# Gate matrices of the dense tokens: from one fp32 product a token to three bf16 products a token

## What is computed

```python
s1 = jnp.einsum('thd,kd->thk', q[:, :, 0], sub_k1)
s2 = jnp.einsum('thd,kd->thk', q[:, :, 1], sub_k2)
v1, i1 = lax.top_k(s1, PEER_TOPK)
v2, i2 = lax.top_k(s2, PEER_TOPK)
...
top_s, top_pos = lax.top_k(cand, PEER_TOPK)
eidx = jnp.take_along_axis(cand_idx, top_pos, axis=-1)   # i1 * 128 + i2
gate = jax.nn.softmax(top_s, axis=-1)
act = jax.nn.gelu(jnp.einsum('thkd,td->thk', expert_u[eidx], xb))
y = jnp.einsum('thk,thkd->td', gate * act, expert_v[eidx])
```

## Time and profile before

| | us |
|---|---|
| three runs | 3722.89, 3715.84, 3708.44 |
| median | 3715.84 |
| span of the profiled execution | 3715.8 |
| its TensorE, busy | 3517.8 (95%) |
| its Vector engine, busy | 2481.2 (67%) |
| its GpSimd, busy | 1842.5 (50%) |
| its ScalarE, busy | 1361.9 (37%) |

### The profile page before, as it was taken

The page is one execution under the profiler, slowest core; times in us unless marked ns, Lnnn a source line. Parts: engine busy times, 40 slices in busy tenths (PEclk is TensorE's granted clock), DMA queues, the critical chain, the costliest instruction groups (busy, mean ns, idle before and its releaser), DMA issues.

```text
span 3715.8 us, 61775 instructions
## 1 busy us (share of the span) xinstructions
PE 3517.8 (95%) x21277; PEld 3348.0 (90%) x21277; DVE 2481.2 (67%) x5400; ACT 1361.9 (37%) x1938; POOL 1842.5 (50%) x1172
## 2 busy tenths in 40 slices
PE   7999999999999999999888689999999999999998
PEld 7999999999999999999773359999999999999998
DVE  3342597777775777775678543679697876777774
ACT  3322343534444333333221353344435353333332
POOL 3434456555655555552541234456565655555551
PEclk9999999999999999999998699999999999999999
DMA  3222367877788999994346322467777879999982
GB/s 131 80 69 91 103 188 247 277 247 262 262 281 274 298 310 313 324 320 154 99 116 179 105 74 91 136 193 249 268 240 277 274 282 277 297 326 311 329 295 97
DMA packets 392484, 812.36 MB, mean 219 GB/s; under 512 B 52104, under 2 KB 249672, under 8 KB 384888
## 3 DMA queue, kind: packets, MB, share of 16 engines
q1 hardware_dynamic: 171600, 458.35, 37.0%
q0 software_dynamic: 64608, 230.73, 18.1%
q10 hardware_dynamic: 156048, 120.37, 11.0%
HBM read 695.39 MB, written 112.74 MB: 217 GB/s over the span
## 4 chain that ended last, share of the span: by engine, by line
PE 66%; DVE 16%; DMA 7%; issue 4%; ACT 2%; POOL 2%; SPq 2%; another core or an unknown queue 0%; ACTq 0%; DVEq 0%; POOLq 0%
PE acc L638 42%; PE acc L625 15%; DMA rows<-u_in,expertP 4%; PE misc L774 3%; DVE rows L1838 3%; DMA raw<-slabs_in 2%; POOL w_lo L2274 1%; DVE misc L1773 1%; DVE route L1777 1%; DVE hot_gate L1876 1%; PE misc L814 1%; ACT w_hi L1104 1%; DVE work L1716 1%; DVE keyi L1724 1%; PE misc L843 1%
## 5 line engine op out<-in xcount | busy, mean ns | idle before, releaser
L2274 POOL TENSOR_TENSOR w_lo<-raw,w_hi 128x1024 fp32r<-128x1024 f32 x365 | 892.6, 2446 | 1079.8 <-ACT w_hi L1104 1078.6
L638 PE MATMUL acc<-h_hi,w_hi 128*128 128x416 f32 x3072 | 1097.7, 357 | 0.2 <-POOL h_lo L2316 0.2
L638 PE MATMUL acc<-h_lo,w_hi 128*128 128x416 f32 x3072 | 1085.9, 353 | 0.0
L638 PE MATMUL acc<-h_hi,w_lo 128*128 128x416 f32 x3072 | 1081.2, 352 | 0.0
L1104 ACT ACTIVATE w_hi<-raw 128x1024 fp32r<-128x1024 f32 x617 | 653.3, 1060 | 1090.0 <-DMA raw<-slabs_in 1045.4
L638 PEld LDWEIGHTS acc<-h_hi,w_hi 128*128 128x128 f32 x3072 | 581.2, 189 | 8.5 <-POOL h_lo L2316 0.6
L638 PEld LDWEIGHTS acc<-h_hi,w_lo 128*128 128x128 f32 x3072 | 581.9, 189 | 7.4
L638 PEld LDWEIGHTS acc<-h_lo,w_hi 128*128 128x128 f32 x3072 | 581.3, 189 | 3.9
L1955 DVE TENSOR_TENSOR w_lo<-raw,w_hi 128x1024 fp32r<-128x1024 f32 x252 | 325.4, 1291 | 206.1 <-ACT w_hi L1104 205.5
L1838 DVE CUSTOM_DVE_ANT_0 rows<-acc,rows 128x1024 f32<-128x1024 f32 (+1 forms) x224 | 273.4, 1221 | 205.9 <-DMA rows<-u_in,expertP 183.7
L638 PE MATMUL acc<-y_hi,w_hi 128*128 128x416 f32 x1024 | 362.1, 354 | 10.3 <-DVE y_lo L1947 4.3
(11 more groups left out here) (349 smaller groups left out, 5549.4 us busy)
## 6 DMA issues: line engine op xcount, KB each, us to landing
raw<-slabs_in SPq DMA_DIRECT2D x617, 512.0 KB
act_d<-gelu SPq DMA_DIRECT2D x256, 208.0 KB
gate_d<-gout SPq DMA_DIRECT2D x52, 1024.0 KB
abuf<-act_d ACTq DMA_DIRECT2D x32, 1664.0 KB
gbuf<-gate_d ACTq DMA_DIRECT2D x30, 1664.0 KB
unit<-ck_in SPq DMA_DIRECT2D x72, 128.0 KB
vquad<-cv_in SPq DMA_DIRECT2D x64, 128.0 KB
unit<-ck_in ACTq DMA_DIRECT2D x56, 128.0 KB
```

Of the source, the lines that this page charges most:

```text
L638: last = pe.matmul(acc[:, 0, par, 0:ND], w[:, c, :], m(c), start=c == 0 and w is w_hi[r] and m is m_hi, stop=c == KC - 1 and w is w_lo[r])
L2274: pool.tensor_tensor(w_lo[r][:], raw[r][:], w_hi[r][:].bitcast(F32), ALU.subtract).then_inc(lo_done, 1)
```

## The change

`idxT` and `gateT` become bf16, and `gateT` holds three bf16 parts of the gate. `gate_parts`, new and run once in each block after `gateT`'s first part has come, makes parts two and three by subtraction. A bf16 count `iota8` in SBUF, in which each of the numbers 0 to 127 stands eight times, is made once a layer and takes the place of `count_row`. The one-hots are bf16 with the token as the innermost of the free dimensions, so that the 8 tokens of a step are done by one tensor_tensor: two comparisons and three products, five instructions of 128x1024 elements. TensorE reads one token's operands out of them with a step of 8 elements (16 bytes) and adds three products into the same PSUM place. The differences `topd` and `topdS` are now written where the exponential is taken (the names stand for that place).

```diff
-        idxT = take("idxT", [P, 2, ND])
-        gateT = take("gateT", [P, ND])
+        idxT = take("idxT", [P, 2, ND], BF16)
+        gateT = take("gateT", [P, 3, ND], BF16)
+        iota8 = take("iota8", [P, P, TG // 2], BF16)
...
-        hot1 = [take(f"hot1_{r}", [P, HG, P]) for r in range(2)]
-        hot_gate = [take(f"hot_gate{r}", [P, HG, P]) for r in range(2)]
+        hot1 = [take(f"hot1_{r}", [P, P, HG], BF16) for r in range(2)]
+        hot_gate = [take(f"hot_gate{r}", [P, 3, P, HG], BF16) for r in range(2)]
...
-                            last = pe.matmul(misc[:, q, j * P:(j + 1) * P], hot1[par][:, t, :],
-                                             hot_gate[par][:, t, :], start=True, stop=True)
+                            for part in range(3):
+                                last = pe.matmul(misc[:, q, j * P:(j + 1) * P], hot1[par][:, :, t],
+                                                 hot_gate[par][:, part, :, t], start=part == 0, stop=part == 2)
...
-            count_row = misc[:, 3, 0:P]
+            rest = misc[:, 3, 0:P]
...
-                dve.tensor_copy(count_row, iota[:]).then_inc(dve_step, step.up())
...
+            def gate_parts(b):
+                t0 = max(b * P, D0)
+                c0, c1 = t0 - D0, (b + 1) * P - D0
+                gate = misc[:, 2, 2 * P + t0 - b * P:3 * P]
+                left = rest[:, t0 - b * P:P]
+                dve.tensor_tensor(left, gate, gateT[:, 0, c0:c1], ALU.subtract).then_inc(dve_step, step.up())
+                dve.wait_ge(dve_step, step.at)
+                dve.tensor_copy(gateT[:, 1, c0:c1], left).then_inc(dve_step, step.up())
+                dve.wait_ge(dve_step, step.at)
+                dve.tensor_tensor(gateT[:, 2, c0:c1], left, gateT[:, 1, c0:c1], ALU.subtract).then_inc(parts_done, 1)
+                dve.wait_ge(parts_done, n_parts[0] + 1)
+                n_parts[0] += 1
+
             def one_hots(half, t0, par, first):
...
-                dve.tensor_tensor(hot1[par][:], count_row.unsqueeze(1).to_broadcast([P, HG, P]),
-                                  idxT[:, 0, t0:t0 + HG].unsqueeze(2).to_broadcast([P, HG, P]), ALU.is_equal)
-                for t in range(HG):
-                    last = dve.tensor_scalar(hot_gate[par][:, t, :], count_row, idxT[:, 1, t0 + t:t0 + t + 1],
-                                             gateT[:, t0 + t:t0 + t + 1], ALU.is_equal, ALU.mult)
-                last.then_inc(hot_done, 1)
+                of = [P, P, HG]
+                dve.tensor_tensor(hot_gate[par][:, 2], iota8[:], idxT[:, 1, t0:t0 + HG].unsqueeze(1).to_broadcast(of),
+                                  ALU.is_equal).then_inc(dve_step, step.up())
+                dve.tensor_tensor(hot1[par][:], iota8[:], idxT[:, 0, t0:t0 + HG].unsqueeze(1).to_broadcast(of),
+                                  ALU.is_equal)
+                dve.wait_ge(dve_step, step.at)
+                for part in range(2):
+                    dve.tensor_tensor(hot_gate[par][:, part], hot_gate[par][:, 2],
+                                      gateT[:, part, t0:t0 + HG].unsqueeze(1).to_broadcast(of),
+                                      ALU.mult).then_inc(dve_step, step.up())
+                dve.wait_ge(dve_step, step.at)
+                dve.tensor_tensor(hot_gate[par][:, 2], hot_gate[par][:, 2],
+                                  gateT[:, 2, t0:t0 + HG].unsqueeze(1).to_broadcast(of), ALU.mult).then_inc(hot_done, 1)
...
+                dve.tensor_copy(iota8[:], iota[:].unsqueeze(2).to_broadcast([P, P, HG])).then_inc(dve_step, step.up())
+                dve.wait_ge(dve_step, step.at)
```

More of the change, by code:

```diff
@@ L220, in build @@
         topv = take("topv", [P, PH, TOPK])
-        topd = take("topd", [P, PH, TOPK])
         topp = take("topp", [P, PH, TOPK], U32)
@@ L225, in build @@
         route = take("route", [P, 3, PH, TOPK])
+        topd = route[:, 2]
         gsum = take("gsum", [P, 2, PH])
@@ L230, in build @@
         topvS = take("topvS", [P, 1, TOPK])
-        topdS = take("topdS", [P, 1, TOPK])
         toppS = take("toppS", [P, 1, TOPK], U32)
@@ L235, in build @@
         routeS = take("routeS", [P, 3, 1, TOPK])
+        topdS = routeS[:, 2]
         gsumS = take("gsumS", [P, 2, 1])
         qS = take("qS", [P, 2, SR])
-        idxT = take("idxT", [P, 2, ND])
-        gateT = take("gateT", [P, ND])
+        idxT = take("idxT", [P, 2, ND], BF16)
+        gateT = take("gateT", [P, 3, ND], BF16)
+        iota8 = take("iota8", [P, P, TG // 2], BF16)
         y_tail = take.end
@@ L395, in build @@
         slotT_done, hot_done, gate_mm = sem("slotT_done"), sem("hot_done"), sem("gate_mm")
-        gate_taken = sem("gate_taken")
+        gate_taken, parts_done = sem("gate_taken"), sem("parts_done")
         gate_stored = [sem(f"gate_stored{r}") for r in range(2)]
@@ L1297, in peer @@
                     act.wait_ge(gate_exp_in, B + 1)
-                    act.activation(route[:, 2], topd[:], ACT.Exp).then_inc(gate_exp_done, 1)
+                    act.activation(route[:, 2], topd, ACT.Exp).then_inc(gate_exp_done, 1)
                     if b == NDB - 1:
@@ L1312, in peer @@
                     act.wait_ge(act_step, step.at)
-                    act.activation(gateT[:, lo - D0:t0 + P - D0], misc[:, 2, 2 * P + lo - t0:3 * P], ACT.Copy).then_inc(
+                    act.activation(gateT[:, 0, lo - D0:t0 + P - D0], misc[:, 2, 2 * P + lo - t0:3 * P], ACT.Copy).then_inc(
                         slotT_done, 1)
@@ L1921, in peer @@
                     dve.wait_ge(slotT_done, B + 1)
+                    gate_parts(b)
                     for r in range(STEPS_OF[b]):
@@ L2260, in _ @@
             n_traw = [0]
+            n_parts = [0]
             peer(0)
```

## The result

The changed kernel takes 4280.54 us (median of 4 runs, 4272.39 to 4289.49) against 3716.28 for the kernel before (4 runs, 3708.44 to 3722.89): a ratio of 1.1525, 95% interval 1.1497 to 1.1554. That is 564 us slower. The forecast was 69 us slower, within 3685 to 3850. The sign was right; the size was wrong by a factor of eight.

What follows compares the result with a forecast made beforehand. Prediction: TensorE nearly bounds the steps (6.31 us), with a ring of 7.0 us in late ones. Six long blocks by (4.7 + 4.0 + 1.5) = 61, block 0 twice 8, small ones 0: +69 on 3715.8, 3785 us; range 3685 to 3850.

Steps and rivals of the forecast that it cites:

- TensorE's part: Gate products in each step: 24 bf16 products at 106 ns, 2.54 us in place of 1.76, +0.78 us a step.
- The rival at 0.06: Gate products: a strided load of one element per line costs twice 106 ns, +3.3 us a step, 4015 us; chance 0.06.
- the late steps: Last 10 of a block's 16 steps: 7.4 us a step against 7.0, +0.4 each, 4 us a block.
- The Vector engine's part: One-hots of each step: five bf16 instructions at two elements a cycle, 3.1 us in place of 3.70, -0.6.
- the rival without double rate: One-hots: bf16 doesn't go at two elements a cycle, 5.8 us a step, 3940 us in all; chance 0.06.
- The lock: One-hots with two SBUF inputs beside GpSimd's `w_lo` stretch by 0 to 2.4 us; 1.4 taken for late steps.
- the early steps: First 6 of a block's 16 steps: TensorE sets them, one-hots fit; +0.78 us each, 4.7 us a block.
- the rival at 58 ns: Gate products: 2-byte loads are shorter, 58 ns, but the lock takes the gain; 3715 us, within 3700 to 3735; chance 0.17.
- the ring: Late-step chain through gates, GpSimd, row transfer and Vector engine: 21.0 us over three steps, 7.0 a step; 22.4 after.
- The faster rival: Gate products at 58 ns and `w_lo` seldom meeting the one-hots: -4.8 us a block, 3684 us in all; chance 0.13.
- start: Start of a block: `gate_parts` delays the first one-hots, 1.5 us in six blocks, about 1 in block 0's two.
- small ones: Around the routing: `iota8` copies +2 us, removed copy of L1799 -2 us, together 0.

Runs made afterwards that it cites:

- both_packed: Changed kernel, but TensorE reads both operands of each gate product as 128 contiguous bf16 elements (products of the wrong elements): 3774.62 us.
- pairs_inside: Changed kernel with tokens in pairs innermost, so TensorE's step is 4 bytes in place of 16: 3764.74 us; run once more, 3767.28 us.
- pairs against their control: Token-pairs kernel with GpSimd's subtraction in the s stages replaced by a zero fill, 3616.52 us; control, the kernel before with the same fill, 3653.38 us.
- moving_packed: Changed kernel with only the moving operand of the gate products read contiguous, the stationary one keeping its 16-byte step (wrong elements): 3749.10 us.

## Why the prediction failed, step by step

**TensorE's part: wrong, and decisive.** The step at fault is "I take 106 ns: 24 x 0.106 = 2.54 us, +0.78 a step". Measured: 235 ns, 5.65 us, +3.89. Two things in it were wrong and leaned opposite ways. The 106 ns of the earlier trace rows were read on 4-byte elements and don't carry over; 128 bf16 columns load behind a 58 ns product, so the lower bound from slab columns, 58, was exactly the packed price (both_packed). But all rows I bounded from read contiguous operands, and the moving operand's step of 16 bytes multiplies the price by four (235 against 58), above my upper end of 110. I had the step only in a sentence of its own and in a rival of 0.06, and there on the stationary operand, which costs 8 ns. By the Trainium skill's rule ("SBUF — State Buffer", Specifications (TRN2)), two hits in a 16-byte line are enough for full bandwidth, and each crossing to another line pays. The second half has the direction right for this case, and the 1.84 ns for each 16 bytes touched agree with it. The first half does not fit: a step of 8 bytes, with two elements in each line, already doubles the price (118 ns). The measurement decides.

**The rival at 0.06** (212 ns, 4015 us) came nearest. It is off by 266 us: the product (235 for 212) gives 57, the clock, which no line of the prediction considered, 165; and it let the late steps hide 0.7 us each.

**The clock: left out.** I took the slab as 4.55 us whatever stood beside it. At 24 slow products it takes 6.1, 165 us, because part of each slab runs at granted 0.50, 347 ns a matmul in place of 188. The slabs alone, which the prediction named as the sign of a cause outside its sum, stayed unchanged at 72.72 us for sixteen. The sign was badly chosen: the cause outside the sum was in the slabs inside the steps.

**The Vector engine's part: right in kind.** Each instruction takes 683 ns where nothing stretches it, as long as half as many fp32 elements, 3.1 us a step. So the rival without double rate is out. The copy for `iota8` took 0.69 us, not 1.2.

**The lock: mechanism right, its consequences not, and hidden in the change itself.** L1891 reached 2,875 ns, `w_lo` has a median of 2.40 as before. In the kernel after, TensorE's steps of 11.9 us cover it: only the first step of a block waits, 12.5 us in eight blocks, near the forecast 1.5 and 1. Where products are cheap the lock shows: for 58 ns I had 3715 us, and the pairs measured 3765 and 3767. The 1.4 us for the stretching were not too low: 4.69 - 3.21 = 1.5 us a step on average in the changed kernel, 4.18 - 3.21 = 1.0 in the pairs. What was too low is what it leads to. I thought the early steps free of it, and they aren't: in the six long blocks of pairs_inside the first six distances have a mean of 7.18 us against 6.51 before, where the rival at 58 ns had 0.37 less, not 0.67 more. The other nine have 7.20 against 6.67, 0.53 more where it had 0.07. (These 6.67, with the transposes in them, also say that the 7.0 of the late steps, read from one turn of the ring, was too high.) And the clock, which falls in the pairs' steps and never in those of before, wasn't in the sum.

**The faster rival.** At 58 ns and without the lock I had -32 us; pairs against their control measured -37. That is in part luck: in both kernels of that pair GpSimd's instruction was also shorter, 953 ns in place of 2,400, which the sum of the ring didn't have.

**Late and early steps, start, small ones** could not be seen apart in a kernel bound by TensorE alone. The removed copy of L1799 agrees in direction: 46.7 us of idle time before the transposes against 51.5.

What stays open is why the granted clock falls while TensorE is shown busy with slow products. The runs show only that it does with 16 and with 24 of them in a step, and that packing the moving operand alone all but ends it: moving_packed has 36 of 675 us of its steps at 0.50, and TensorE waits in them. What sets the 1.84 ns for each 16 bytes stays open too.

## What to carry to other kernels

Before a layout makes an element-wise engine fast, look at who else reads it: the token-innermost layout was to shorten the Vector engine's one-hots from 3.7 to 3.1 us a step (beside GpSimd they took 4.7), and it made TensorE's stream four times as long, and TensorE was the bound. A price bounded by rows that share the size but not the access pattern is no bound; ask for the step of the moving operand first. And an instruction with two SBUF inputs beside a busy GpSimd costs more than its median says: price it by its mean, stretched ones included, and by what waits behind it.

## What the runs showed of the hardware

- The stream of a moving bf16 operand of 128 columns costs 58 ns at a step of 2 bytes, 59 at 4, 118 at 8 and 235 at 16. The stationary operand at 16 bytes costs 8 ns more than packed.
- At half the granted clock the products at 2 and 4 bytes go from 56 and 57 to 107 ns from start to start; those at 8 and 16 bytes stay at 118 and 234.
- In steps with 16 or 24 products of 235 ns the granted clock fell from 1.00 to 0.50 in the midst of work that the profile shows unbroken (263 of 913 us and 508 of 1148 us at 0.50), and slabs went from 4.55 to 6.1 us and over. With 24 products of 118 ns it was 20 of 721 us.
- A two-input Vector instruction on bf16, with one input a row of 2, 4 or 8 elements repeated, took 0.68 us at 1024 elements, as long as an fp32 one at 512.
- One comparison in a step, moved from PSUM to SBUF beside GpSimd's subtraction, cost some 25 us in 104 steps; its median stayed at 1.22 us and its maximum went from 1.23 to 3.39.
